# Index scores in a two-block transformer kernel: two heads per insertion, products alternating between the halves of the rows

## What is computed

```python
def block_fn(args):          # 128 queries at a time; IDX_HEADS = 8, IDX_DIM = 64
    ql, qi, wi, t0 = args
    s_idx = jax.nn.relu(jnp.einsum('btjd,bsd->btjs', qi.astype(f32), k_idx_f))
    s_idx = jnp.einsum('btjs,btj->bts', s_idx, wi.astype(f32))
    s_idx = jnp.where(causal[None], s_idx, -jnp.inf)
    _, idx = lax.top_k(s_idx, topk)
```

## Time and profile before

| | |
|---|---|
| median of three runs | 1374.83 us (1370.41 to 1375.87) |
| the profiled execution | 1375.14 us |
| its span, first to last instruction | 1373.0 us |
| PE busy | 1323.6 us (96%) |
| DVE busy | 854.1 us (62%) |
| ACT busy | 577.0 us (42%) |
| POOL busy | 218.9 us (16%) |
| granted TensorE clock, mean | 0.983 of full speed |

### The profile page before, as it was taken

The page is one execution under the profiler, slowest core; times in us unless marked ns, Lnnn a source line. Parts: engine busy times, 40 slices in busy tenths (PEclk is TensorE's granted clock), DMA queues, the critical chain, the costliest instruction groups (busy, mean ns, idle before and its releaser), DMA issues.

```text
span 1373.0 us, 16091 instructions
## 1 busy us (share of the span) xinstructions
PE 1323.6 (96%) x5982; PEld 1030.1 (75%) x5982; DVE 854.1 (62%) x1498; ACT 577.0 (42%) x871; POOL 218.9 (16%) x173
## 2 busy tenths in 40 slices
PE   7999988999999999999999999999999989989996
PEld 6777656888888888888888876787778755658885
DVE  6455753798887378738853644589785356653342
ACT  5344645544433134323322453224673255553321
POOL 2322211000000000000000033240006411114550
PEclk9999998999999999999999999999999989999998
DMA  5211101132222222222322141321222200002411
GB/s 194 92 62 62 62 31 62 34 120 92 92 97 106 104 92 92 92 94 103 109 93 92 62 154 38 132 107 62 92 92 93 92 32 31 32 31 92 153 62 61
DMA packets 17788, 116.52 MB, mean 85 GB/s; under 512 B 1984, under 2 KB 2240, under 8 KB 4544
## 3 DMA queue, kind: packets, MB, share of 16 engines
q1 hardware_dynamic: 16320, 108.35, 22.4%
q10 hardware_dynamic: 1408, 7.37, 1.4%
HBM read 111.52 MB, written 4.19 MB: 84 GB/s over the span
## 4 chain that ended last, share of the span: by engine, by line
PE 93%; DVE 4%; ACT 1%; issue 1%; DMA 1%; DVEq 0%; ACTq 0%; SPq 0%
PE PG L355 19%; PE PG L356 19%; PE PG L357 19%; PE PX L505 5%; PE PX L786 3%; PE PX L440 2%; PE PG L440 2%; PE PG L439 2%; PE PX L439 2%; PE PG L441 2%; PE PX L441 2%; PE PG L815 2%; PE PX L682 1%; PE PX L825 1%; PE PX L519 1%; PE PX L623 1%
## 5 line engine op out<-in xcount | busy, mean ns | idle before, releaser
L355 PE MATMUL PG<-XH,WH 128*128 128x512 f32 x992 | 392.9, 396 | 2.7 <-DVE XL L1588 2.7
L335 POOL TENSOR_TENSOR WL<-RAW,WH 128x512 fp32r<-128x512 f32 x160 | 215.6, 1379 | 1121.6 <-ACT WH L873 1121.6
L356 PE MATMUL PG<-XL,WH 128*128 128x512 f32 x992 | 386.2, 389 | 0.0
L357 PE MATMUL PG<-XH,WL 128*128 128x512 f32 x992 | 386.2, 389 | 0.0
L873 ACT ACTIVATE WH<-RAW 128x2048 fp32r<-128x2048 f32 x100 | 191.4, 1914 | 355.1 <-PE PG L357 244.6
L355 PEld LDWEIGHTS PG<-XH,WH 128*128 128x128 f32 x992 | 186.2, 188 | 48.8 <-issue 10.0
L356 PEld LDWEIGHTS PG<-XL,WH 128*128 128x128 f32 x992 | 186.3, 188 | 39.1 <-issue 1.9
L357 PEld LDWEIGHTS PG<-XH,WL 128*128 128x128 f32 x992 | 186.2, 188 | 38.8
L1324 DVE TENSOR_TENSOR WL<-RAW,WH 128x2048 fp32r<-128x2048 f32 x60 | 137.3, 2288 | 60.8 <-ACT WH L873 60.6
L1075 ACT ACTIVATE Z<-Z 128x512 f32<-128x512 f32 x32 | 20.3, 633 | 165.4 <-DVE Z L1639 165.4
L1623 DVE TENSOR_TENSOR U<-PG,R 128x1024 f32<-128x1024 f32 x32 | 39.2, 1224 | 51.0 <-PE PG L357 45.4
(11 more groups left out here) (313 smaller groups left out, 2078.8 us busy)
## 6 DMA issues: line engine op xcount, KB each, us to landing
RAW<-panels SPq DMA_DIRECT2D x100, 1024.0 KB, 4.7
x_spill<-XT ACTq DMA_DIRECT2D x1, 2048.0 KB, 7.0
XT<-x_spill ACTq DMA_DIRECT2D x1, 2048.0 KB, 7.8
outT<-SQ SPq DMA_DIRECT2D x4, 512.0 KB, 3.0
XT<-xT ACTq DMA_DIRECT2D x2, 512.0 KB, 6.7
XT<-xT SPq DMA_DIRECT2D x2, 512.0 KB, 9.3
RGW<-rgw ACTq DMA_DIRECT2D x1, 1024.0 KB, 4.7
UK<-uk ACTq DMA_DIRECT2D x1, 512.0 KB, 5.7
```

The source lines that it names most:

```text
L335: ins = pool.tensor_tensor(WL[:, s].rearrange("p a b -> p (a b)")[:, piece], RAW[:, s, piece], WH[:, s].rearrange("p a b -> p (a b)")[:, p ...
L355: pe.matmul(o, WH[:, s, c, ms], xh[:, c, :], start=(c == 0), stop=False)
L356: pe.matmul(o, WH[:, s, c, ms], xl[:, c, :], start=False, stop=False)
L357: mm = pe.matmul(o, WL[:, s, c, ms], xh[:, c, :], start=False, stop=(c == DC - 1))
```

## The change

`idx_scores` takes a pair number v instead of a unit. It issues the six products of heads 2v and 2v+1 together: for each of the three parts first the product of the lower half of the rows, then that of the upper half, into the two banks 2v % 4 and 2v % 4 + 1. The table puts the 12 pairs behind every second group of the panels: groups 4, 6, ... 14 of panel 3 and 2, 4, ... 12 of panel 4. From v = 2 a pair waits for the relus of the pair two before it; the low part of the later queries is awaited at v = 1 instead of u = 3. ACT and DVE do the same work in the same order.

```diff
-        IDX_PLACES = {3: {4 + n: n for n in range(12)}, 4: {2 + n: 12 + n for n in range(12)}}
+        IDX_PLACES = {3: {4 + 2 * n: n for n in range(6)}, 4: {2 + 2 * n: 6 + n for n in range(6)}}
...
-            def idx_scores(u):
-                qb, j = u // IDX_HEADS + 1, u % IDX_HEADS
+            def idx_scores(v):
+                qb, pair = v // 4 + 1, v % 4
                 n = (qb + 1) * P
-                rows = slice((j % 2) * HD, (j % 2) * HD + HD)
-                if u == 0:
+                if v == 0:
                     pe.wait_ge(once("idx_split"), 2)
-                if u == 3:
+                if v == 1:
                     pe.wait_ge(once("idx_split"), 3)
-                if u >= 4:
-                    pe.wait_ge(once("idx_relu"), u - 3)
-                qh, ql = (q[rows, j // 2, qb * P:(qb + 1) * P] for q in (QIH, QIL))
-                pe.matmul(PX[:, u % 4, 0:n], qh, KIH[rows, 0:n], start=True, stop=False)
-                pe.matmul(PX[:, u % 4, 0:n], qh, KIL[rows, 0:n], start=False, stop=False)
-                pe.matmul(PX[:, u % 4, 0:n], ql, KIH[rows, 0:n], start=False, stop=True).then_inc(once("idx_s"), 1)
+                if v >= 2:
+                    pe.wait_ge(once("idx_relu"), 2 * v - 2)
+                for k, (q, key) in enumerate(((QIH, KIH), (QIH, KIL), (QIL, KIH))):
+                    for m in range(2):
+                        rows = slice(m * HD, (m + 1) * HD)
+                        mm = pe.matmul(PX[:, (2 * v + m) % 4, 0:n], q[rows, pair, qb * P:(qb + 1) * P], key[rows, 0:n],
+                                       start=(k == 0), stop=(k == 2))
+                        if k == 2:
+                            mm.then_inc(once("idx_s"), 1)
...
-                for u in IDX_PLACES.get(k, {}).values():
+                for u in [2 * v + m for v in IDX_PLACES.get(k, {}).values() for m in range(2)]:
```

More of the change, by code:

```diff
@@ L1797, in _ @@
             for t in range(3, 7):
-                for u in IDX_PLACES.get(t, {}).values():
+                for u in [2 * v + m for v in IDX_PLACES.get(t, {}).values() for m in range(2)]:
                     idx_add(u)
```

## The result

| | before | changed |
|---|---|---|
| median, beside each other | 1371.29 us (1367.83 to 1375.87, six runs) | 1360.72 us (1358.22 to 1361.59, six runs) |
| ratio | | 0.9916, 95% interval 0.9898 to 0.9934 |
| profiled execution | 1375.14 us | 1360.46 us |
| its span | 1373.0 us | 1358.3 us |
| mean granted clock | 0.983 | 0.989 |

The kernel became 0.84% faster. That is 11.5 us by the ratio (9.1 to 14.0) and 10.6 us by the medians; 11.2 us had been forecast. The absolute time is 3.2 us under the forecast of 1363.9, and also under the 1361.2 to 1366.6 that the prediction gave to its likeliest case.

What follows compares the result with a forecast made beforehand. TensorE was taken to bound panels 3 and 4. Fewer passages (5.0 us) plus products on two halves at once (6.2 us) gave 11.2 us off 1375.14, forecasting 1363.9 us, with a range of 1360.5 to 1370.3.

Steps and rivals of the forecast that it cites:

- likeliest case: Whole kernel: the full saving arrives, 1363.9 us with the half spread of runs, 2.7 us, to either side; chance 0.78.
- What bounds the kernel: Panels 3 and 4: TensorE is busy in every microsecond at the upper clock, so shortening its sequence saves time.
- Term 1: Panels 3 and 4: 12 insertions instead of 24 save 12 passages between full and 64 rows at 0.42 us, 5.0 us.
- Term 2: Index products in panels 3 and 4: two halves run fully side by side, saving 6.2 us; bounds 0 and 6.2.
- The sum: TensorE in panels 3 and 4: 5.0 + 6.2 = 11.2 us saved, all arriving at the end.
- The two signals: Last two products of each pair: both signal; by the skill's rule 0.3 us less saving, by the rows none.
- ACT and DVE: Relus and additions in twos in panels 3 and 4: no TensorE wait; evacuation at most 0.1 us later.
- The base: Whole kernel: the saving is subtracted from the profiled execution, 1375.14 us, 0.3 above the median of 1374.83.
- A: Index pairs: the halves run in turn for fp32r, only 5.0 us saved, 1370.1 us; chance 0.08.
- B: Index pairs: the halves overlap only in part, 8.6 us saved, 1366.5 us; chance 0.06.
- C: Inside insertions: each change of halves costs a passage, 12.0 us added in all, slower at 1382.1 us; chance 0.03.
- D: Attention stage: stretches at half clock give back 3 to 5 us of TensorE's saving, 1367 to 1369 us; chance 0.05.

Runs made afterwards that it cites:

- dummy kernel: Changed kernel with the 48 products of panel 3 issued twice, one time ahead of it (10.88 us added): 1372.91 us, ratio 1.0010 to the kernel before.
- full rows: Kernel before, 24 insertions of one head, with all 128 rows of queries and keys in each index product instead of 64: 1364.01 us, ratio 0.9951.
- pairs in 24 insertions: Changed kernel with 24 insertions instead of 12, each taking half the columns of a pair: 1369.24 us, ratio 0.9972 to the kernel before.
- four heads in spread places: Changed kernel with two pairs in each of 6 insertions, behind groups 4, 7, 11, 15 of panel 3 and 4, 9 of panel 4: 1362.00 us.
- four heads in even places: Changed kernel with two pairs of heads in each of 6 insertions, behind every fourth group: 1362.18 us, ratio 0.9928 to the kernel before.
- the run with six and six: Kernel with four heads per insertion, but six products of the two lower heads first, then six of the two upper: 1366.34 us, one execution.

## Why the prediction came out as it did

**What bounds the kernel.** Right. TensorE was busy without a gap in panels 3 and 4, and what left them left the total: dummy work of the same length brought the old time back, to within -1.2 and +4.0 us.

**Term 1, fewer passages.** Right, with its size. 0.42 us for each insertion was read from single periods; full rows gave 0.40 over all 24, the pairs in 24 insertions an estimated 0.42, and four heads in spread places 0.36. Twelve at 0.40 are 4.8 us, where 5.0 was forecast; with term 2 that makes 11.0, beside 10.9 measured.

**Term 2, side by side.** Right in size (6.2 us forecast, 6.2 measured by putting both heads on one half), and its mechanism is shown: two halves side by side. That the order must alternate, which the change takes for granted, the prediction did not examine. With three products of one half ahead of three of the other it was the same. The rows hinted at this: L815 issues one head and then the other as well, two records each, and their records start in pairs.

**The sum.** 11.2 us forecast for the panels, 10.9 measured. The two panels had been expected at 15.8 and 17.2 us and took 16.05 and 17.30. The 0.3 us by which the sum missed lie mostly outside the insertions. The sum counted every product of the panels with the 0.227 us of panel 5. In both kernels those that follow one another between the insertions have 0.231 on average (829.44 to 830.38 us in the changed kernel, for instance, is four in 0.94 us), and 71 of them are 0.3 us. The two signals are not the cause: an insertion with 512 keys took the same 0.90 us with two signals and with one, 850.25 to 851.15 us in the changed kernel and 856.42 to 857.32 before, and over all insertions the averages differ by 6 to 8 ns. The rule of the Trainium skill ("TensorE: Matmul & The Clock Gate", "The cost: per-tile semaphore tail") has about 26 ns for the second signal. This case does not show them in the time of TensorE, and here the measurement decides.

**ACT and DVE.** Right: no wait of TensorE in the two panels, and the evacuation as early as before. With four heads in even places the wait did appear.

**The base.** This is the step that failed. The sum was taken off the profiled execution, 1375.14 us, with the median of three, 1374.83, as its support. The six runs beside the changed kernel had a median of 1371.29 us, and larger groups of the same kernel 1370.3 to 1373.0. The base was thus 2 to 5 us too high, 3.9 by the six. The forecast was too high by the 3.2 us seen, since the saving by the medians was 0.6 under the 11.2. The prediction also took the spread of three runs, 2.7 us to either side, as if that base were its middle. So its likeliest case ended at 1361.2, above the measured median; the low end of the range, 1360.5, lies only 0.2 us under the median, and two of the six runs were below it.

What the runs show in place of that step is that one and the same kernel has several times, each with its mean granted clock. Of 59 executions of the kernel before, 13 at 0.983 took 1374.7 to 1376.0 us, 18 at 0.985 took 1372.0 to 1373.5, 12 at 0.988 took 1369.6 to 1370.6, and 6 at 0.990 took 1366.9 to 1367.7; the rest lie between. The profiled execution had 0.983: it was one of the slowest kind, and the figure stood beside it.

**The rivals.** A (in turn), 1370.1 us: excluded by the timeline. B (in part): excluded, the panels hold the full 6.2 us. C (each change of halves a passage): excluded by the same rows. D (stretches at half clock) came with the other sign, for which the prediction has half a sentence. In the first profile of the changed kernel 2.1 us were missing ahead of the panels and 1.7 behind, beside a mean clock of 0.989 instead of 0.983. All ten executions of the changed kernel had 0.987 to 0.990, while 31 of the 59 of before had 0.983 or 0.985, and 8 of the 10 of the dummy kernel. So the higher clock is no accident of one profile, and the code alone does not bring it, since the dummy kernel has the same code. Nor does a shorter time alone: the full rows, 9.5 us shorter in the panels, had 0.984 to 0.987 in six executions. At the same mean clock (0.987, 0.988, 0.989 and 0.990) the changed kernel was 9.1 to 9.7 us faster than before. The mean also counts dips at which TensorE has little to do, so it is a rough measure, and how much of the 10.6 us comes from the clock stays open. That the total came so close to the forecast saving is therefore in part luck; the 10.9 us inside the panels are not.

**What stays open.** Why the clock dips at other places, and less often, in one execution than in another of the same program, and why the changed kernel sees fewer dips. The clock is read here, not set: no run held it fixed.

## What to carry to other kernels

Count how often TensorE goes from products of full rows to products of half the rows and back; here each visit cost about 0.4 us with 256, 384 or 512 columns alike, so gather small products, as far as the engines behind them keep up. Two products of 64 rows on different halves, into different banks, cost here what one costs, with at most three others between them. For a change worth less than 1%, take the base from many runs and look at the granted clock of the one that was profiled. Judge the change by the stretch that it touches, whose length repeated to 0.02 us while the total moved by several microseconds.

## What the runs showed that was not expected

TensorE does not start products strictly in the order of the program: a product for the other half of the rows started past three that were waiting for the first half (832.71 us in the run with six and six). And the middle pair of an insertion had the same pitch of 0.12 us with 128 columns as with 256: cutting the products from 256 to 128 columns took 0.08 us off an insertion, not the 0.17 that half the columns would be.
